# A fused two-block forward pass on one core: sums of the modulations regrouped between TensorE and VectorE, and several orders rewritten

## The reference

```
mods = split(c_act @ w_ada[i] + b_ada[i], 6)      # sh1, sc1, g1, sh2, sc2, g2
u = x * (1 + sc1) + sh1
y = gla_mixer(u)            (layer 0)   or   chunk_attention(u)   (layer 1)
x = layer_norm(alpha * x + (1 + g1) * y)
u = x * (1 + sc2) + sh2
y = square(relu(u @ w1)) @ w2
x = layer_norm(alpha * x + (1 + g2) * y)
```

## Time and profile before

| | |
|---|---|
| median of 3 runs | 1041.35 us (1040.75 to 1042.88) |
| the profiled execution | 1044.56 us |
| its span, in which all times of the trace lie | 1042.8 us |
| TensorE | 1002.2 us busy, 96% |
| VectorE | 802.6 us busy, 77% |
| ScalarE | 508.2 us busy, 49% |
| GpSimd | 69.9 us busy, 7% |
| read from memory | 225.82 MB, 218 GB/s |

### The profile page before, as it was taken

The page is one execution under the profiler, slowest core; times in us unless marked ns, Lnnn a source line. Parts: engine busy times, 40 slices in busy tenths (PEclk is TensorE's granted clock), DMA queues, the critical chain, the costliest instruction groups (busy, mean ns, idle before and its releaser), DMA issues.

```text
span 1042.8 us, 16753 instructions
## 1 busy us (share of the span) xinstructions
PE 1002.2 (96%) x6806; PEld 899.4 (86%) x6806; DVE 802.6 (77%) x1254; ACT 508.2 (49%) x684; POOL 69.9 (7%) x147
## 2 busy tenths in 40 slices
PE   7999989999998899999999999899999999999996
PEld 7987768989987698888999988799988989999995
DVE  3499888998898878668886666768884858777776
ACT  3494436334434665726344343634456456555563
POOL 3101220110000111000100000200000000000000
PEclk9999999999999999999999999999999999999998
DMA  9968775799999375443875655263343435665551
GB/s 351 382 224 309 286 272 202 282 352 356 322 330 340 136 265 185 137 156 126 334 272 175 214 197 182 71 227 133 122 162 121 167 131 189 189 206 191 184 194 68
DMA packets 35180, 227.96 MB, mean 219 GB/s; under 512 B 4224, under 2 KB 4352, under 8 KB 10272
## 3 DMA queue, kind: packets, MB, share of 16 engines
q1 hardware_dynamic: 25232, 167.01, 45.8%
q0 software_dynamic: 9872, 59.89, 15.4%
HBM read 225.82 MB, written 1.06 MB: 218 GB/s over the span
## 4 chain that ended last, share of the span: by engine, by line
PE 68%; DVE 17%; issue 6%; ACT 5%; DMA 2%; POOL 0%; POOLq 0%; DVEq 0%; ACTq 0%
PE ps L450 61%; DVE ada_raw L1517 5%; DVE weight_lo L1501 5%; ACT weight_hi L1072 3%; DMA ada_raw<-ada 2%; DVE mlp_relu L1898 1%; PE ps L845 1%; PE ps L952 1%; PE ps L835 1%; PE ps L834 0%; PE ps L665 0%; DVE act_lo L1590 0%; PE ps L717 0%; DVE dev L1653 0%; DVE dev L1646 0%
## 5 line engine op out<-in xcount | busy, mean ns | idle before, releaser
L1501 DVE TENSOR_TENSOR weight_lo<-weight_raw,weight_hi 128x2048 fp32r<-128x2048 f32 (+2 forms) x192 | 310.0, 1618 | 65.3 <-ACT weight_hi L1072 65.2
L1072 ACT ACTIVATE weight_hi<-weight_raw 128x2048 fp32r<-128x2048 f32 (+2 forms) x168 | 298.7, 1788 | 52.6 <-PE ps L450 41.8
L450 PE MATMUL ps<-act_hi,weight_hi 128*128 128x256 f32 x1336 | 317.8, 281 | 3.4 <-DVE act_lo L1590 1.8
L450 PE MATMUL ps<-act_lo,weight_hi 128*128 128x256 f32 x1336 | 312.5, 277 | 0.0
L450 PEld LDWEIGHTS ps<-act_hi,weight_hi 128*128 128x128 f32 x1336 | 250.2, 187 | 12.9 <-issue 8.2
L450 PEld LDWEIGHTS ps<-act_lo,weight_hi 128*128 128x128 f32 x1336 | 250.4, 187 | 3.2 <-issue 1.0
L450 PE MATMUL ps<-act_hi,weight_lo 128*128 128x256 f32 x1336 | 174.5, 277 | 0.0
L450 PEld LDWEIGHTS ps<-act_hi,weight_lo 128*128 128x128 f32 x1336 | 161.5, 187 | 0.4 <-DVE weight_lo L1501 0.2
L450 PE MATMUL ps<-weight_hi,mlp_hi 128*128 128x512 f32 x256 | 101.2, 395 | 4.6 <-DVE mlp_lo L1904 4.6
L1256 ACT ACTIVATE mlp_hi<-mlp_relu 128x512 fp32r<-128x512 f32 x32 | 20.3, 635 | 170.4 <-DVE mlp_relu L1898 166.9
L450 PE MATMUL ps<-weight_hi,mlp_lo 128*128 128x512 f32 x256 | 100.8, 394 | 0.0
(11 more groups left out here) (320 smaller groups left out, 1320.3 us busy)
## 6 DMA issues: line engine op xcount, KB each, us to landing
weight_raw<-weights SPq DMA_DIRECT2D x144, 1024.0 KB, 5.1
ada_raw<-ada POOLq DMA_DIRECT2D x48, 1024.0 KB, 6.7
weight_raw<-weights SPq DMA_DIRECT2D x23, 512.0 KB, 3.8
row_g<-ln_rows POOLq DMA_DIRECT2D x4, 512.0 KB, 4.3
row_b<-ln_rows POOLq DMA_DIRECT2D x4, 512.0 KB, 5.4
att_bias<-rel_bias POOLq DMA_DIRECT2D x16, 128.0 KB, 3.7
square<-gates POOLq DMA_DIRECT2D x3, 512.0 KB, 4.6
dev<-x_in SPq DMA_DIRECT2D x1, 1024.0 KB, 5.5
```

Of the source, the lines that this page charges most:

```text
L450: return e.matmul(o, a, b, start=start, stop=False, skip_group_check=True)
L1072: e.activation(weight_hi[h][:, 0:size], weight_raw[r][:, 0:size], ACT.Copy).then_inc(hi_full[h], 1)
L1501: ins = e.tensor_tensor(weight_lo[h][:, a + at:b + at], weight_raw[r][:, c], weight_hi[h][:, c].bitcast(F32), ALU.subtract)
```

## The change

**Ring of four.** `ada_raw` gets a fourth slot, `ada_acc` is gone.

**First input.** TensorE computes the shift alone (8 matmuls, 16 passes a tile), and only for tiles 0 to 4. VectorE sums the scale of each tile by one 128x1024 multiplication with accumulation, and for tiles 5 to 7 the shift by another (`feature_sums`). The host lays the chunks out for it. The first product of the second weight chunk begins with tile 5 instead of 6, ScalarE's splits stand at tiles 1, 4, 6 instead of 1, 3, 5. GpSimd waits for VectorE's sums (and for TensorE's, for the first five) and loads the ninth chunk only when the eighth has landed; SyncE's fourth weight chunk waits for six tiles' sums.

```diff
-N_RAW, N_SPLIT, N_ADA_RING = 3, 3, 3
+N_RAW, N_SPLIT, N_ADA_RING = 3, 3, 4
...
+                    if j == N_RAW:
+                        e.wait_ge(ada_used, KT - 2)
...
-                for x in range(2):
-                    c = slice(x * P, (x + 1) * P)
-                    for k in range(U_ROWS, KT):
-                        mm(ps[:, 6 + f % 2, c], raw[:, k, c], c_act[:, k:k + 1].broadcast_to([P, P]),
-                           start=(x == 0 and k == U_ROWS))
-                e.wait_ge(ada_used, f + 1)
-                for x in range(2):
-                    last = mm(ps[:, 6 + f % 2, x * P:(x + 1) * P], ada_acc[:, (2 * f + x) * P:(2 * f + x + 1) * P], ones_sq[:, :])
+                for k in range(KT):
+                    last = mm(ps[:, 6 + f % 2, 0:P], raw[:, k, :], c_act[:, k:k + 1].broadcast_to([P, P]), start=(k == 0))
...
-            first = ((0, work_tiles(W["gk"], 1), P, 2), (1, work_tiles(W["q0"]), 256, 6),
+            first = ((0, work_tiles(W["gk"], 1), P, 2), (1, work_tiles(W["q0"]), 256, 5),
                      (2, [(q1_ps[:, n, :], 4) for n in range(2)], 256, 7))
             for f in range(KT):
-                first_mods(f)
+                if f < U_TILES:
+                    first_mods(f)
...
-                if k in (1, 3, 5):
-                    split_hi(k // 2)
+                if k in (1, 4, 6):
+                    split_hi((1, 4, 6).index(k))
...
+                def feature_sums(f):
+                    slot = f % N_ADA_RING
+                    e.wait_ge(ada_full[slot], 16 * (f // N_ADA_RING + 1))
+                    for x in range(0 if f >= U_TILES else 1, 2):
+                        raw = ada_raw[slot][:, x * D:(x + 1) * D]
+                        ins = e.scalar_tensor_tensor(out=raw, in0=raw, scalar=1.0, in1=c_row[:, :], op0=ALU.mult,
+                                                     op1=ALU.mult, accum_out=mod(0, x, f))
+                    ins.then_inc(ada_used, 1)
...
-                e.wait_ge(c_done, 1)
+                e.wait_ge(c_row_in, 1)
                 for f in range(KT):
+                    feature_sums(f)
                     if f:
                         residue(f - 1)
+                    mods_of_tile(f)
                     if f in (2, 5, 7):
                         split_lo((2, 5, 7).index(f))
```

```diff
             split_lo(7)
-            ada_chunk()
             gate_product(0)
...
             split_lo(8)
             gate_product(1)
-            ada_chunk()
             split_lo(9)
...
             ada_chunk()
             split_lo(15)
+            ada_chunk()
             gated_head(3)
             out_residue(2)
-            ada_chunk()
...
             add_bias(0, 3)
-            ada_chunk()
+            add_bias(0, 4)
...
+            split_lo(J_OUT0 + 3)
             out_residue(3)
-            split_lo(J_OUT0 + 3)
-            add_bias(0, 4)
```

```diff
-                    if (m, i) in ((0, 4), (0, 13), (1, 8)):
-                        gate_columns(3 if m else 1 + (i == 13))
-                    if m == 1 and 3 <= i < 7:
+                    if (m, i) in ((0, 4), (1, 8)):
+                        gate_columns(2 * m + 1)
+                    if m == 0 or 3 <= i < 7:
+                        ada_chunk()
+                    if m == 0 and i == 4:
                         ada_chunk()
                     split_lo(up_chunk(m, i) + 3)
-                    if m == 0 and i < 4:
-                        ada_chunk()
-                    elif m == 0:
-                        ada_chunk()
-                        if i % 2 == 0 and i < n_blocks - 2:
-                            ada_chunk()
```

```diff
+                ada_chunk()
                 split_lo(J_ATT + 6 + slot)
-                if slot < 4:
-                    ada_chunk()
```

```diff
+                e.wait_ge(*emptied(W["mv0"]))
+                high(0, 0)
+                low(0, 0)
+                high(0, 1)
+                keep_busy("mv1", 6)
+                turn(3, 1)
+                keep_busy("mv1", 3)
+                high(1, 0)
+                low(1, 0).then_inc(chunk_done, 1)
+                high(1, 1)
+                low(0, 1).then_inc(v_done, 1)
+                low(1, 1).then_inc(chunk_done, 1)
```

More of the change, by code:

```diff
@@ L43 @@
 HALF = 512
-U_ROWS, U_BUSY = 3, 12
+U_BUSY = 12
+U_TILES = 5
 LINE, STAYING, MOVING = 256, 128, 64
@@ L586, in turn, with v_half @@
                     last.then_inc(x_turned, 1)
[L588 to L594 removed]
+            def v_half(j, t, w, ready=None, turn_at=None):
                 ts = slice(t * P, (t + 1) * P)
@@ L609, in v_half @@
                     e.wait_ge(lo_full[(j + c) % N_SPLIT], (j + c) // N_SPLIT + 1)
-                    if turn_at and turn_at[1] == 2 * c + 1:
-                        if before:
-                            before()
-                        turn(turn_at[0], 1)
                     for k in range(4):
```

113 lines of the change are left out of this document (65 added, 48 removed).

## The result

The changed kernel takes 1032.89 us (median of 4 runs, 1031.41 to 1033.63), the kernel before in runs beside it 1042.12: a ratio of 0.991, 95% interval 0.989 to 0.9929. It is faster by 9 us, half of the 18.2 that I had forecast, and outside of my range, whose upper end was 1030.0. A second set of runs gave 1031.8 against 1043.91, a ratio of 0.9891 (0.9875 to 0.9908): 12 us. Of the 3 us between the two sets, 1.8 lie in the kernel before and 1.1 in the changed one.

A forecast was written before the change was run, and what follows sets the result against it. The prediction took the kernel to be bound by TensorE, busy 1002.2 of 1042.8 us, so only its waits and lower clock could go. Terms 3.0 + 1.9 + 1.9 + 7.5 + 1.3 + 2.6 = 18.2 gave 1023.1 us, range 1018.5 to 1030.0.

The forecast's parts named there:

- A: First input: tile 7's chunk lands at 34.5 and the stage ends at 46.7; gain 3.0 us (0.7 to 4.0).
- B: GLA's first gate products: both sums gone from ahead of them, so TensorE's waits go; gain 1.9 us (1.2 to 1.9).
- C: GLA's end: wait ahead of `out0_half` removed, w_out's fourth chunk split no longer behind two sums; 1.9 us (0.5 to 2.2).
- D: First MLP: TensorE's 4.59 us wait at `hidden(15)` and the half clock after it go; gain 7.5 us (7.2 to 7.9).
- the turn behind it: Behind the first MLP: nine idle products where TensorE waits anyway; 0 us (-0.5 to 0.5).
- E: Attention: sums fit VectorE's idle time ahead of `split_lo` and no longer delay `att_out_lo`; gain 1.3 us (-2.7 to 1.9).
- F: Mixer's values: TensorE's 2.56 us wait and half clock give way to a shorter wait; gain 2.6 us (1.0 to 3.5).
- The lower clock: First input: rival with A only 0.7, 1025.4 us, chance inside the forecast's 0.72; failure sign from 40 to 47 us.
- The new wait for `weight_lo` in the MLP: MLP or attention: new TensorE waits for `weight_lo` would show the prediction wrong.
- The check by the second MLP: First MLP's gain checked against the second MLP, which does the same products: 184.6 - 177.4 = 7.2 us.
- a payback in the attention's late slots: Attention's late slots: 1.32 us of room for a 2.3 us sum, total gain only 12.9, 1028.5 us; chance 0.10.
- nothing moves: Whole kernel: each wait is replaced by the next of the same size, no change; chance 0.03.

The follow-up runs named there:

- w0_early: Changed kernel with SyncE's first weight chunk waiting for the landing of the first modulations chunk instead of VectorE's first sum: 1029.61 us.
- both mends: Changed kernel with late modulations chunks held until the seventh weight chunk lands, and the first weight chunk loaded once the first modulations chunk lands: 1025.08 us, ratio 0.9818.
- hold_late_sums: Changed kernel with GpSimd loading the twelfth and later modulations chunks only when the seventh weight chunk has landed: 1027.65 us.
- gated_back: Kernel with both mends, with TensorE's wait for the last gated head put back ahead of the w_out product's third quarter: 1028.02 us.
- sums_back: Changed kernel with the first MLP's 20 sums and the attention's four back in their old places: 1040.19 us.
- mlp_behind: Changed kernel with the sums of the first MLP's loop behind the second split instead of ahead of it, same number: 1033.04 us.

## Why the prediction was wrong

By its terms, with the mean of two executions of each kernel from the table:

| term | forecast | measured | what it was |
|---|---|---|---|
| A, first input | 3.0 | 0.3 | the first weight chunk's late landing |
| B, GLA's first gate products | 1.9 | -1.2 | the collision; 2.3 without it |
| C, GLA's end | 1.9 | 2.6 | right, low |
| D, first MLP | 7.5 | 7.0 | right |
| the turn behind it | 0 | -1.3 | 0.8 norm's chain, 0.5 open |
| E, attention | 1.3 | 1.5 | right |
| F, mixer's values | 2.6 | 2.0 | right; 2.7 or 1.3 by before's clock |

The measured terms add to 10.9 us, 7.3 short of the forecast, and between the 9.2 and 12.1 us of the medians.

**A** failed at the sentence that the loads would be issued early. The last chunk of the modulations landed near its forecast: tile 7's at 32.67 to 35.06 in the five executions, where I had 34.5. What failed is VectorE's path, which I had put at 36.9 without a wait: in the first profile it began at 13.16 instead of 11.64 and stood still for 1.67 us for the input of its first split and 3.62 and 0.85 us for TensorE's shifts. I did not follow the three weight chunks, whose loads wait for VectorE's sums. The first sum ended at 10.6 us before and ends at 14.4 now, since it is longer and waits for `c_row`; with it the first weight chunk's load moved. Queued behind TensorE's wait for it were the shifts of tiles 3 and 4, and behind these VectorE. `w0_early` shows it; with both mends the forecast's 46.7 is met (46.79), and there the first sum for tile 7 starts at 34.41. I had also counted "4.0 earlier" against the execution of before that was the slower of two by 1.45. Over all executions the term is smaller still: the mean of five is 50.1, that of before's two as well.

In A I also misread a row. The load issued at 35.26 is that of the tenth chunk; tile 7's is the eighth, and was issued at 28.70:

```profile
28.70 0.53 POOL L2289 DMA_DIRECT2D ada_raw<-ada  x1 [3.84 <-PE ps L450]
```

It took 11.2 us to its landing at 39.91, with the third and fourth weight chunks and the ninth of the modulations on the way beside it. In the changed kernel it is issued at 26.84, only 1.9 us earlier, and takes 5.8 us. So the early landing comes mostly from what no longer stands beside it (the fourth weight chunk and the ninth of the modulations now wait), and not from an early issue. The sum of bytes by rate, on which the 34.5 rests, does not hang on that row.

The lower clock, which I held for a rival, came in every execution of the changed kernel. It lay ahead of 38 us in the first profile, in waits, in the shifts and in products ahead of the last, and not in the last products as I had feared; in the second it reached to 40.8, 0.8 us into the stretch that I had named as a sign of being wrong. I take its cost to be under the 3.3 us that I named, but no run shows its size.

**B** failed at the sentence (it stands under A) that the two sums ahead of GLA cost nothing, since VectorE is idle there. That was right for VectorE: its idle time there went from 7.16 to 3.07 us. But a sum frees a slot, and a free slot lets GpSimd start a load; with the fourth slot, three more loads of 1 MB (issued at 39.87, 45.77 and 48.61) were under way when SyncE's seventh chunk was issued at 55.27. I had priced moved instructions and not what they release. This is the largest error, 3.1 of the 7.3 us by which the terms miss, and 3.5 by the mean of the six executions; `hold_late_sums` shows it.

**C** was right for the wrong price: the removed wait alone is worth 2.9 us in the changed order (`gated_back`), since the sums moved ahead would have made it longer. The change also moves ScalarE's split of the fourth chunk of w_out ahead of its highs of the last two heads, which the list of changes above leaves out; what that is worth no run shows.

**D** was right in its place, cause and size (`sums_back`, `mlp_behind`); VectorE's busy time in that stage is 155.69 us, near the forecast's 157. What I left out is that the next stage gives 1.3 us back, where I had said 0 (-0.5 to 0.5): TensorE ends nearer to VectorE's split, from which the norm runs 7.0 us whatever TensorE does. That is 0.8 of it, and the cause of the rest is open. The new wait for `weight_lo` in the MLP, which I had named as a sign of being wrong, is there, at 0.5 us. The check by the second MLP could not show that, as it compared the two MLPs alone.

**E and F** were right; `sums_back` shows E, while F has no run of its own, only its stage in the table. The rival of a payback in the attention's late slots did not come: 92.9 us with eight sums.

Of the rivals, "nothing moves" was the nearest to what happened in B and at the turn: another wait took the place of the one removed. I had given it 0.03 for the kernel as a whole, and had not asked it of each term, where it belongs.

## What to carry to other kernels

When an instruction that frees a buffer is moved earlier, follow the load that it lets go, and ask which other transfer is under way then: an idle stretch of the engine says nothing about the queues. When a sum or a step gets longer or starts later, list everything that waits on its semaphore, the loads of other engines above all. And a stall taken from one stage is only a gain up to the next fixed chain behind it. Where a row is to tell when a load was issued, count the loads up to it: the one nearest in time need not be the one that is waited for.

## What the runs showed of the hardware

TensorE begins a launch at 1.2 GHz (its first idle products start 0.21 to 0.22 us apart, and 0.11 to 0.12 later on), and when the clock rises does not follow from the kernel alone. Both executions of the kernel before started their products at 4.08 and 4.09 us and were at 2.4 GHz from 7.96. Eleven executions of changed kernels started at 4.60 to 4.62 us, and rose between 7.6 and 10.6 us (the changed kernel at 10.56 and 10.20, the same first products in `mlp_behind` at 7.62). The row `c_row` comes up to 1.4 us later by that (13.13 in the changed kernel, 11.75 in `mlp_behind`). Likewise, behind the same wait of 4.6 to 4.8 us ahead of `mlp_lo`, TensorE stayed at 1.2 GHz for 6.8 us in one execution of the kernel before and for 3.4 in the other, and behind the same 2.6 us ahead of the mixer's second rows for 3.4 us in the one and not at all in the other. And the load of the first weight chunk, 0.5 MB among the same other loads, takes 4.4 to 8.3 us in the five executions above. A sum made against a single profiled execution carries all that as an error of 1 to 3 us.
